# First mix of a two-block float32 transformer: a fifth low part by the adding DMA, and the rotation's cosine product written in its PSUM bank

## The reference

```python
h = rms_norm(x, norm1_g)
proj = h @ w_in                                   # 1024 -> 2560
q, k, v, u = jnp.split(proj, [512, 1024, 1536], axis=-1)
q = apply_rope(rms_norm(q, q_norm_g), cos, sin)   # 8 heads of 64
k = apply_rope(rms_norm(k, k_norm_g), cos, sin)   # xf * cos + rotated halves * sin
attn = causal softmax attention over the 256 tokens (q, k, v)
conv = conformer_conv(u)                          # GLU, causal depthwise convolution of 31 taps,
                                                  # LayerNorm over channels, swish
x = x + concatenate([attn, conv]) @ w_out
x = x + (silu(rms_norm(x) @ w_gate) * (rms_norm(x) @ w_up)) @ w_down
```

## Time and profile before

| | |
|---|---|
| median of 3 runs | 1283.84 us (1283.7 to 1285.47) |
| the profiled execution's own time | 1285.46 us |
| its span | 1283.6 us |
| TensorE (PE) busy with matmuls | 1268.8 us, 99% |
| TensorE loading weights (PEld, beside matmuls) | 1082.2 us, 84% |
| VectorE (DVE) busy | 836.1 us, 65% |
| ScalarE (ACT) busy | 683.0 us, 53% |
| GpSimd (POOL) busy | 108.5 us, 8% |
| moved by DMA | 239.14 MB, mean 186 GB/s |

### The profile page before, as it was taken

The page is one execution under the profiler, slowest core; times in us unless marked ns, Lnnn a source line. Parts: engine busy times, 40 slices in busy tenths (PEclk is TensorE's granted clock), DMA queues, the critical chain, the costliest instruction groups (busy, mean ns, idle before and its releaser), DMA issues.

```text
span 1283.6 us, 18155 instructions
## 1 busy us (share of the span) xinstructions
PE 1268.8 (99%) x6988; PEld 1082.2 (84%) x6988; DVE 836.1 (65%) x1123; ACT 683.0 (53%) x909; POOL 108.5 (8%) x130
## 2 busy tenths in 40 slices
PE   9989999999999999999999999999999999999998
PEld 8878888888888888787888888888888877888886
DVE  7898655565655548898765556655565776675552
ACT  7796544443544435756564444544454665564441
POOL 1861000000000000022000000000002120000000
PEclk9999999999999999999999999999999999999999
DMA  9946765563755544527575554675553754475540
GB/s 312 258 98 197 254 205 196 196 216 115 244 196 192 185 153 132 164 89 239 197 233 184 185 187 161 204 255 196 195 186 127 242 160 165 150 239 183 184 145 33
DMA packets 178446, 239.14 MB, mean 186 GB/s; under 512 B 4671, under 2 KB 158031, under 8 KB 178384
## 3 DMA queue, kind: packets, MB, share of 16 engines
q1 hardware_dynamic: 171360, 224.25, 52.9%
q0 software_dynamic: 6288, 12.85, 4.1%
q10 hardware_dynamic: 736, 1.19, 0.3%
HBM read 237.22 MB, written 1.05 MB: 186 GB/s over the span
## 4 chain that ended last, share of the span: by engine, by line
PE 94%; DVE 2%; ACT 2%; POOL 1%; issue 1%; DMA 0%; DVEq 0%; SPq 0%; POOLq 0%; ACTq 0%
PE psum L1285 23%; PE psum L1179 15%; PE psum L1181 15%; PE psum L1180 15%; PE psum L1293 12%; PE psum L1306 2%; PE psum L1246 2%; PE psum L1245 2%; PE psum L1244 2%; PE psum L1310 1%; PE psum L1517 1%; PE psum L1408 1%; PE psum L1565 1%; ACT ws L756 1%; PE psum L1530 1%
## 5 line engine op out<-in xcount | busy, mean ns | idle before, releaser
L1970 DVE TENSOR_TENSOR w_lo<-raw,w_hi 128x2048 fp32r<-128x2048 f32 x193 | 439.7, 2284 | 84.7 <-ACT w_hi L511 83.4
L511 ACT ACTIVATE w_hi<-raw 128x2048 fp32r<-128x2048 f32 x211 | 401.1, 1906 | 37.0 <-PE psum L1181 13.7
L1285 PE MATMUL psum<-t_both,w_hi 128*128 128x512 f32 x1280 | 304.8, 390 | 0.0
L1285 PEld LDWEIGHTS psum<-t_both,w_hi 128*128 128x128 f32 x1280 | 237.4, 188 | 47.4
L1179 PE MATMUL psum<-w_hi,f_hi 128*128 128x512 f32 x488 | 193.4, 396 | 0.0
L1181 PE MATMUL psum<-w_hi,f_lo 128*128 128x512 f32 x488 | 190.6, 391 | 0.0
L1180 PE MATMUL psum<-w_lo,f_hi 128*128 128x512 f32 x488 | 190.6, 391 | 0.0
L1179 PE MATMUL psum<-w_hi,t_both 128*128 128x512 f32 (+2 forms) x448 | 162.9, 364 | 0.0
L1293 PEld LDWEIGHTS psum<-t_both,w_lo 128*128 128x128 f32 x1280 | 158.9, 192 | 3.1
L630 ACT ACTIVATE ws<-psum 128x512 f32<-128x512 f32 x40 | 23.9, 597 | 257.0 <-PE psum L1293 257.0
L1293 PE MATMUL psum<-t_both,w_lo 128*128 128x256 f32 x1280 | 159.8, 283 | 0.0
(11 more groups left out here) (218 smaller groups left out, 1299.1 us busy)
## 6 DMA issues: line engine op xcount, KB each, us to landing
raw<-in_ffn_wg SPq DMA_DIRECT2D x44, 1024.0 KB, 5.7
raw<-in_ffn_wu SPq DMA_DIRECT2D x44, 1024.0 KB, 5.3
raw<-in_ffn_wd SPq DMA_DIRECT2D x44, 1024.0 KB, 5.0
raw<-in_even_w_in SPq DMA_DIRECT2D x12, 1024.0 KB, 5.2
raw<-in_odd_w_in SPq DMA_DIRECT2D x12, 1024.0 KB, 5.3
raw<-in_w_gate SPq DMA_DIRECT2D x11, 1024.0 KB, 5.7
raw<-in_w_up SPq DMA_DIRECT2D x11, 1024.0 KB, 5.5
raw<-in_w_down SPq DMA_DIRECT2D x11, 1024.0 KB, 5.1
```

Of the source, the lines that this page charges most:

```text
L511: nc.scalar.activation(w_hi[:, n % SLOTS, 0:w], raw_of(n)[:, 0:w], ACT.Copy).then_inc(hi_done, 1)
L1285: mm = nc.tensor.matmul(bank[b + c][:, :], wh[:, k, c * P:(c + 1) * P], t_both[:, k, :, :].rearrange("p a s -> p (a s)"), start=k == 0 and ...
L1970: nc.vector.tensor_tensor(w_lo[:, n % SLOTS, 0:w], raw_of(n)[:, 0:w], w_hi[:, n % SLOTS, 0:w].bitcast(F32), ALU.subtract).then_inc(lo_done, 1)
```

## The change

**Fifth low part.** Unit 6 joins `LOW_ADDED`: ScalarE writes its negative high part, GpSimd issues a fifth adding DMA, VectorE does not split it. The load of unit 9, which uses unit 6's raw buffer, now waits for that negation and no longer for VectorE.

**Rotation in the bank.** `rope_in_place` takes the place of `rope_parts` in this stage. `rope_begin` makes the two half products with the sine alone. The product with the cosine is made later, by `rope_sum` or `rope_end`, and is written in place in the PSUM bank. The sum then reads one tensor in PSUM and one in SBUF. The bank is free only after that sum. For queries the sum comes in two halves, one for each tile of tokens: the first counts for `roped`, the second for `bank_free`, and `turned` on TensorE waits for both.

**Orders.** TensorE makes `turn(2)` before `tile(9, 0)` and no longer behind `turned(8)`. The lists of ScalarE, GpSimd and VectorE place taps, negations, copies and roots elsewhere. The taps that each engine makes stay the same. The diff, without ScalarE's list and the rest of VectorE's:

```diff
@@ -328,7 +328,7 @@
-        low_in = [sem(f"low_in{i}") for i in range(4)]
+        low_in = [sem(f"low_in{i}") for i in range(5)]
@@ -427,7 +427,7 @@
-        LOW_ADDED = (7, 8, 9, 10)
+        LOW_ADDED = (6, 7, 8, 9, 10)
...
@@ -1120,18 +1118,19 @@
                         inv_root(st[:, root_at(r):root_at(r) + 8])
 
                     pool.wait_ge(params_ok, 2)
+                    add(1)
+                    low_part(6)
+                    add(2)
+                    low_part(7)
+                    add(7)
+                    root(0)
+                    low_part(8)
                     add(5)
-                    low_part(7)
+                    root(1)
+                    low_part(9)
                     add(2)
-                    root(0)
-                    add(5)
-                    low_part(8)
-                    root(1)
-                    add(3)
-                    low_part(9)
-                    add(1)
                     root(2)
-                    add(5)
+                    add(4)
                     root(3)
                     low_part(10)
                     add(9)
@@ -1813,6 +1812,8 @@
                         pe.wait_ge(rope_kept, r)
+                    if r % 2:
+                        pe.wait_ge(bank_free[ph["bank"][u]], left[u])
                     turn_rope(V, units[u][3], 7)
 
@@ -1898,10 +1899,10 @@
                 turn(1)
                 turned(6)
                 tile(8, 1)
+                turn(2)
                 tile(9, 0)
                 spread_sums(0, 0)
                 turned(8)
-                turn(2)
                 values(0)
                 scores(4)
                 turn(3)
@@ -2217,6 +2218,26 @@
                 dve.wait_ge(bank_free[b], ph["left"][j])
                 return r, c_, s_, qr[:, r % 2, :, :].rearrange("p t (h d) -> p t h d", d=dim)
 
+            def rope_in_place(ph, j, tab):
+
+                _, _, _, role = ph["units"][j]
+                r = nx(roped) - 1
+                if r:
+                    dve.wait_ge(roped, r)
+                b, (t2, qr) = ph["bank"][j], (ph["views"][n] for n in ("t2", "qr"))
+                x = bank[b][:, :].rearrange("p (t h d) -> p t h d", t=T, d=64)
+                cos, sin = (tab[:, :, 64 * i:64 * i + 64].unsqueeze(2).broadcast_to([P, T, 4, 64]) for i in range(2))
+                s_ = t2.rearrange("p (t h d) -> p t h d", t=T, d=64)
+                nc.vector.tensor_tensor(s_[:, :, :, 0:32], x[:, :, :, 32:64], sin[:, :, :, 0:32], ALU.mult)
+                at = step(nc.vector.tensor_tensor(s_[:, :, :, 32:64], x[:, :, :, 0:32], sin[:, :, :, 32:64], ALU.mult))
+
+                def rest():
+
+                    dve.wait_ge(dve_step, at)
+                    link(nc.vector.tensor_tensor(x, x, cos, ALU.mult))
+                    return x
+                return r, rest, s_, qr[:, r % 2, :, :].rearrange("p t (h d) -> p t h d", d=64)
+
             def rope_unit(ph, j, tab):
 
                 role = ph["units"][j][3]
@@ -2334,22 +2355,28 @@
                     nc.vector.scalar_tensor_tensor(out=s8, in0=s8, scalar=1.0 / 64, in1=eps_col[:, :], op0=ALU.mult, op1=ALU.add).then_inc(ms_ready, 1)
 
                 def rope_begin(j):
-                    parts[j] = rope_parts(ph, j, qk_rope[:, ph["units"][j][3][3], :, :])
+                    parts[j] = rope_in_place(ph, j, qk_rope[:, ph["units"][j][3][3], :, :])
 
                 def rope_sum(j):
-                    r, c_, s_, dst = parts[j]
-                    link(nc.vector.tensor_tensor(c_, c_, s_, ALU.add))
+                    r, rest, s_, dst = parts[j]
+                    nc.vector.tensor_tensor(s_, rest(), s_, ALU.add).then_inc(bank_free[ph["bank"][j]], 1)
 
                 def rope_end(j):
-                    r, c_, s_, dst = parts[j]
+                    r, rest, s_, dst = parts[j]
+                    b = ph["bank"][j]
+                    if r % 2:
+                        x = rest()
                     if r >= 2:
                         dve.wait_ge(rope_T, r - 1)
                     if r % 2:
-                        nc.vector.tensor_tensor(dst, c_, s_, ALU.add).then_inc(roped, 1)
+                        nc.vector.tensor_tensor(dst[:, 0], x[:, 0], s_[:, 0], ALU.add).then_inc(roped, 1)
+                        nc.vector.tensor_tensor(dst[:, 1], x[:, 1], s_[:, 1], ALU.add).then_inc(bank_free[b], 1)
+                        dve.wait_ge(bank_free[b], ph["left"][j])
                         return
+                    dve.wait_ge(bank_free[b], ph["left"][j])
                     dve.wait_ge(rstd_ready, roots + r + 1)
                     per = st[:, root_at(r):root_at(r) + 8].rearrange("p (t h) -> p t h", t=T).unsqueeze(3).broadcast_to([P, T, 4, 64])
-                    nc.vector.tensor_tensor(dst, c_, per, ALU.mult).then_inc(roped, 1)
+                    nc.vector.tensor_tensor(dst, s_, per, ALU.mult).then_inc(roped, 1)
 
                 def rooted_maxima(h):
 
@@ -2397,62 +2424,60 @@
                 dve.wait_ge(params_ok, 2)
                 split_to(4)
                 glu(1)
+                split_to(5)
+                taps(7)
+                split_to(6)
                 taps(2)
-                split_to(5)
-                split_to(6)
-                taps(4)
-                split_to(7)
-                taps(3)
+                lam_sums()
+                taps(2)
                 setup()
-                taps(3)
-                lam_sums()
-                taps(1)
+                taps(2)
                 glu(3)
                 taps(1)
                 mean_square(0)
                 rope_begin(4)
-                taps(1)
                 rope_sum(4)
-                taps(6)
+                taps(5)
                 rope_end(4)
+                taps(2)
                 mean_square(1)
                 taps(1)
                 rope_begin(5)
-                taps(1)
                 rope_end(5)
-                taps(3)
+                taps(5)
                 mean_square(2)
                 rope_begin(6)
-                taps(1)
                 rope_sum(6)
...
```

More of the change, by code:

```diff
@@ L839, in mix_first @@
                 keep_pt(L, 2)
+                taps(2)
+                exps(L, 4)
                 taps(1)
                 keep_pt(L, 3)
-                taps(1)
-                exps(L, 4)
-                taps(1)
                 exps(L, 5)
```

62 lines of the change are left out of this document (32 added, 30 removed).

## The result

Over 20 runs each the changed kernel took 1286.82 us as median (1285.82 to 1288.69) and the kernel before 1284.60 (1283.35 to 1285.66). The ratio is 1.0018 with a 95% interval of 1.0012 to 1.0024: slower by 2.3 us, between 1.5 and 3.1. That is within the 0.2% that the prediction called no change, but on the other side of the forecast, and outside its range, which ended at 1283.6.

What follows compares the result with a forecast made beforehand. TensorE's waits in the first mix, mainly for a VectorE sum, were taken as the bound. A 2.0 us earlier spread plus the 0.45 us turn gave 2.5 us off the median 1283.84: 1281.3 us, range 1280.0 to 1283.6.

Steps and rivals of the forecast that it cites:

- The rotation: Unit 5's sum on VectorE no longer stands behind GpSimd, so TensorE's wait before the transposes goes: 2.25 us less 0.1.
- The queue of transfers: DMA engines serve loads and additions in order of arrival; unit 6's addition lands at 46.4, before TensorE needs it at 47.26.
- Rival A: Additions and later-issued loads take turns; unit 6's addition lands near 48.9, leaving only the turn's gain: 1283.4 us; chance 0.13.
- Rival D: Additions become the bound: unit 9's lands at 76.6, the spread comes at 79.5; 1286.8 us, slower; chance 0.08.
- hidden: ScalarE's added negation of 1.90 us, ahead of unit 7's load for which it waited 2.09 us, costs nothing.
- Unit 4's power: On GpSimd behind seven additions of taps, ending at 47.6; its scaling ends at 48.3, 1.8 us before TensorE wants it.
- Rival E: GpSimd's seven additions stand behind VectorE, the power ends near 51, unit 4's turn waits 1.5 us: 1282.3 us; chance 0.12.
- From the scores to the spread: VectorE's list from 58.1 sums to 15.8 us, freeing unit 8's bank at 74.0; spread 2.0 us earlier than 76.03.
- Rival C: TensorE's half clock after the gap at 84.7 to 88.1 us does not come: 1280.5 us; chance 0.16.
- the turn: Head 2's turn on TensorE, 0.45 us, moved before tile 9 into waiting time; gain at the first values rises to 2.45 us.

Runs made afterwards that it cites:

- four parts: The changed kernel without the fifth addition, unit 6 split by VectorE again; 1284.71 us, ratio 0.9997 to the kernel before.
- rotation alone: The kernel before with only the rotation in the bank and TensorE's wait for that bank; 1283.58 us, ratio 0.9990.
- four parts and the bank first: The changed kernel with four added low parts and unit 8's rotation moved ahead on VectorE; 1282.95 us, ratio 0.9989 to the kernel before.
- without the new orders: The kernel before with rotation in the bank, unit 8's rotation moved ahead, and head 2's turn ahead of tile 9; 1281.69 us, ratio 0.9974.
- high part of unit 9 late: The changed kernel with ScalarE's high part of unit 9 moved behind the copies of unit 5, no load held; 1288.80 us, ratio 1.0029.
- turn back: The changed kernel with the turn of head 2 moved back behind the transposes of unit 8; 1287.91 us, ratio 1.0027 to the kernel before.
- changed kernel again: The changed kernel, unedited, measured and profiled once more; 1287.84 us, ratio 1.0024 to the kernel before.

## Why the prediction was wrong

**The rotation** was right in mechanism: half sums of 0.4 us beside busy GpSimd, no wait before the transposes of unit 5, and a bank that is free later.

**The queue of transfers** is the step that failed: "In order of arrival: loads 34.2 to 40.2, unit 6's addition to 45.7, landed 46.4". It landed at 50.1. The trace of before was read as arrival order because in 44 to 49 us the addition ran alone. It ran alone because the load behind it was issued late, at 46.72, and moved its first packets only after 48.75. When a load has packets to move beside it, be it issued just ahead (unit 9's) or behind (w_out), the two alternate by packets, and against w_out's long packets an addition is down to a third of its rate. Rival A had this mechanism but priced it as an even share with one load (48.9 us, 1283.4) and got 0.13. Rival D had the measured number, 1286.8, by luck: its late addition was unit 9's, and before tile 9 TensorE did not wait. The rows at hand could have told more: the prediction itself counted the engines full from 34 to 69 us, so any addition in that stretch could meet a load.

**What the lateness costs** was not in the sum. Three prices came with it: the wait of 3.3 us, the low clock behind it (1.2 us in the first record), and the slowed load of unit 9, before which ScalarE stood 1.4 us in one record and 5.2 in another. The prediction had "hidden" for everything on ScalarE, by durations, and did not ask what stands behind a high part whose load is late.

**Unit 4's power.** "Its user, the scaling of unit 4, ends at 48.3": it ended at 51.1. GpSimd's seventh addition waited for ScalarE's tap behind that same high part. Rival E had the place, not the cause; the late tile 6 hid it.

**From the scores to the spread** the length was right, the start was not. The sum was 15.8 us from 58.1; measured are 15.75 from 62.26. The 4.1 us are tile 6 at 50.19 for 47.26 and the 1.2 us of low clock behind it, and with them the gain of 2.0 became a loss of 2.0 (78.06 for 76.03). The mean came at 94.68, past the 93.5 that the prediction had set as its limit. But the working also shows what was not drawn from it: in the kernel before the same stretch ran from 61.7 to 76.0, 14.2 us. The change made VectorE's list before the spread 1.5 us longer: 0.8 by the rotation in the bank and 1.0 by the scaling of unit 6 beside GpSimd (1.68 us for 0.68), less a wait of 0.27. Even on time, as in the runs with four parts (75.47) and with the rotation alone (73.41), TensorE stood 2.2 us before the spread.

**Clock.** Rival C had the low clock as a matter of one gap near the end. It can belong to the price of any longer wait: the 2.2 us wait in the run with the rotation alone had 1.5 us of low clock behind it. Not every such wait has: the 2.25 us before the transposes of unit 5 in the kernel before were followed by a clock of 1.00. C's gap near the end did keep the full clock in both records of the changed kernel (1.00 from 80 to 116 us).

**The parts together**, as medians against the kernel before: rotation alone 1.3 us faster; with the turn and the new orders, four parts, 0.4 (within its interval of no change); the fifth addition 2 to 3.3 us slower on top, though about 0.4 (within its interval of no change) when it is put alone into the kernel before, where it hides behind a stall. The forecast added two gains, rotation and turn, and took the addition and the new orders for free. The addition was not, and by the run with four parts and the bank first (1282.95 us, for 1281.69 without the new orders) the new orders were not either, though those intervals overlap.

## What to carry to other kernels

When a DMA is added to a full queue, look at what will be issued behind it, not only at what is ahead, and compare packet sizes: a transfer in short packets loses against one in long packets. When a stall is removed from an engine's list, find the next release on that same list at once; here moving one release ahead of two taps, a mean square and the reciprocals gave 2.6 us, twice what removing the stall had given, about 1.5 of it low clock that no longer followed a wait. A load that is slowed costs whatever stands behind its first reader in program order.

## What the runs showed of the hardware

- Two DMA queues with work in both moved equal numbers of packets in three stretches of 3 us (345 and 344; 198 and 198; 195 and 198), whether their packets were of equal length or one queue's four times as long.
- An addition did not start sharing at once: issued at 32.98, none of its packets moved between 36 and 37.5 us, while the load of unit 8 did.
- A sum of one PSUM and one SBUF operand was not held by GpSimd's additions (0.42 us for 128x256). The sum of two SBUF tensors took 0.69, 1.69 and 2.91 us in three places, and the scaling out of SBUF, which the change left as it was, 0.69 and 1.68.
- A wait of 3.3 us was followed by 1.2 GHz in one execution, and one of 2.9 us in another by none; one of 2.14 to 2.24 us before the spread by 1.2 GHz in three records (four parts, rotation alone, high part of unit 9 late) and by none in two (turn back, changed kernel again).
